# Expert rows through DRAM: tokens fetched by indirect DMA, results stored as rows and gathered back

## The reference, cut to what matters

```python
def moe_swiglu(h, router, w_gu, w_down):
    t = h.reshape(-1, shp[-1])                      # 256 tokens x 1024
    logits = (t @ router).astype(F32)
    top_v, top_i = lax.top_k(logits, TOP_K)         # 2 of 8 experts
    gates = jax.nn.softmax(top_v, axis=-1)
    combine = jnp.sum(jax.nn.one_hot(top_i, N_EXPERTS, dtype=F32) * gates[..., None], axis=1).astype(t.dtype)
    y = jnp.zeros_like(t)
    for e in range(N_EXPERTS):
        y = y + combine[:, e:e + 1] * swiglu(t, w_gu[e], w_down[e])
    return y.reshape(shp)
```

## Time and profile before

| | |
|---|---|
| median of 3 runs | 1613.47 us (1613.42 to 1613.71) |
| the profiled execution | 1617.29 us |
| its span, first to last instruction | 1615.5 us, mean granted TensorE clock 0.941 |
| PE busy | 1431.4 us (89%) |
| DVE, ACT, POOL busy | 892.8, 728.6, 91.0 us |
| DMA | 263.96 MB, mean 163 GB/s |
| eight expert passes | 1114.7 to 1590.3 us |
| in them: PE, DVE, ACT busy | 452.5, 383.9, 338.3 of 475.5 us, DMA share 0.82, 288 GB/s |

### The profile page before, as it was taken

One profiled execution on the slowest core, in us unless ns is written; L12 is line 12 of the kernel. 1 busy time (PEld: TensorE's weight loads), 2 busy tenths in 40 slices (PEclk: granted clock), 3 DMA queues, 4 the chain that ended last, 5 costly groups with the idle time before them and its releaser, 6 DMA issues.

```text
span 1615.5 us, 23095 instructions
## 1 busy us (share of the span) xinstructions
PE 1431.4 (89%) x8308; PEld 1150.2 (71%) x8308; DVE 892.8 (55%) x1387; ACT 728.6 (45%) x1076; POOL 91.0 (6%) x90
## 2 busy tenths in 40 slices
PE   5599978799889999999979945988999999999996
PEld 1377646356658888888848844667898888888884
DVE  0521276764352332233343486755887887887785
ACT  2322353454332321222132462543677677676774
POOL 2200010000030100011011010010000000000000
PEclk9699979899979999999988967998999999999998
DMA  8255544245212332223202510022887887887883
GB/s 318 77 196 188 202 146 168 104 183 182 79 40 97 115 102 80 91 91 126 83 30 88 167 56 0 1 69 103 303 283 284 304 296 277 303 302 271 300 307 124
DMA packets 69555, 263.96 MB, mean 163 GB/s; under 512 B 8112, under 2 KB 9552, under 8 KB 69360
## 3 DMA queue, kind: packets, MB, share of 16 engines
q1 hardware_dynamic: 68112, 259.55, 46.2%
q10 hardware_dynamic: 720, 2.30, 0.4%
q0 software_dynamic: 656, 1.18, 0.2%
HBM read 261.95 MB, written 1.05 MB: 163 GB/s over the span
## 4 chain that ended last, share of the span: by engine, by line
PE 71%; DVE 13%; ACT 7%; DMA 6%; issue 3%; POOL 0%; DVEq 0%; ACTq 0%; SPq 0%; POOLq 0%
PE ps L544 11%; PE ps L546 11%; PE ps L545 11%; DMA raw<-in_w_dn 3%; DVE wlo L460 3%; PE ps L880 3%; PE ps L884 3%; PE ps L882 3%; ACT whi L455 3%; PE ps L727 3%; PE ps L521 3%; PE ps L860 3%; PE ps L749 2%; PE ps L862 2%; PE ps L861 2%
## 5 line engine op out<-in xcount | busy, mean ns | idle before, releaser
L460 DVE TENSOR_TENSOR wlo<-raw,whi 128x1024 fp32r<-128x1024 f32 (+2 forms) x367 | 481.8, 1318 | 363.5 <-ACT whi L455 357.9
L455 ACT ACTIVATE whi<-raw 128x1024 fp32r<-128x1024 f32 (+2 forms) x367 | 411.8, 1124 | 370.0 <-PE ps L546 153.3
L544 PE MATMUL ps<-hhi,whi 128*128 128x512 f32 (+1 forms) x736 | 285.4, 388 | 40.1 <-POOL hlo L1275 38.7
L546 PE MATMUL ps<-hhi,wlo 128*128 128x512 f32 (+1 forms) x736 | 277.9, 378 | 0.0
L545 PE MATMUL ps<-hlo,whi 128*128 128x512 f32 (+1 forms) x736 | 277.4, 377 | 0.0
L860 PE MATMUL ps<-whi,hs_hi 128*128 128x256 f32 x704 | 207.9, 295 | 16.4 <-DVE wlo L460 12.6
L544 PEld LDWEIGHTS ps<-hhi,whi 128*128 128x128 f32 x736 | 141.7, 193 | 91.4 <-issue 37.2
L862 PE MATMUL ps<-whi,hs_lo 128*128 128x256 f32 x704 | 196.6, 279 | 0.0
L861 PE MATMUL ps<-wlo,hs_hi 128*128 128x256 f32 x704 | 196.6, 279 | 0.0
L545 PEld LDWEIGHTS ps<-hlo,whi 128*128 128x128 f32 x736 | 142.7, 194 | 25.2 <-issue 1.4
L546 PEld LDWEIGHTS ps<-hhi,wlo 128*128 128x128 f32 x736 | 142.7, 194 | 24.2
(11 more groups left out here) (251 smaller groups left out, 1928.2 us busy)
## 6 DMA issues: line engine op xcount, KB each, us to landing
raw<-in_w_gu SPq DMA_DIRECT2D x225, 512.0 KB, 4.4
raw<-in_w_dn SPq DMA_DIRECT2D x80, 704.0 KB, 6.1
raw<-in_w_mod SPq DMA_DIRECT2D x96, 512.0 KB, 4.2
raw<-in_w_fm SPq DMA_DIRECT2D x32, 512.0 KB, 3.4
raw<-in_w_out SPq DMA_DIRECT2D x16, 512.0 KB, 3.7
raw<-in_w_tg SPq DMA_DIRECT2D x8, 512.0 KB, 3.4
raw<-in_w_tv SPq DMA_DIRECT2D x8, 384.0 KB, 3.1
xT<-in_x ACTq DMA_DIRECT2D x1, 2048.0 KB, 12.0
```

The costliest lines, as they stand in the source:

```text
L455: nc.scalar.activation(whi[:, v % H, 0:cols], raw[:, slot, 0:cols], ACT.Copy).then_inc(hi_ready, 1)
L460: nc.vector.tensor_tensor(wlo[:, v % H, 0:cols], raw[:, place(v) % R, 0:cols], whi[:, v % H, 0:cols].bitcast(F32), ALU.subtract).then_inc( ...
L544: nc.tensor.matmul(outp, whs, xh, start=first, stop=False)
L546: return nc.tensor.matmul(outp, wls, xh, start=False, stop=last)
```

## The change

Tokens and results go through two DRAM tensors, and the matrices pair_w, scat and the sum yacc go.

- **h_rows** (256 x 1024): ACT stores both tiles of htm there before the first pass.
- **Slot to token.** tok holds each token's number (with the sign and offset that the constant matrix `before` gives). `slot_tokens(i)` on PE multiplies pair_in by tok, two products of one column, into bank 6, after j = 3 of the pass before; `slots_of(i)` on DVE turns the result into the integers slot_tok.
- **Fetch.** Pool fetches 128 rows of h_rows by indirect DMA into xg, once slot_tok is ready. `gather(i)` on PE now waits for xg and turns it by eight transposes into the same place of PSUM. pair(i + 1) on DVE moves from r == 9 to r == 3; slots_of(i + 1) stands at r == 9.
- **y_rows** (2048 x 1024): ACT stores ys there at the end of each pass, from its own queue, after it has waited for its copy. Its upper half is set to zero early, by Pool from back, before the norm ahead of the experts.
- **Back.** DVE works out slot_at, the two rows of y_rows that each token needs (`rows_of_tokens`), and wdiag, four diagonal matrices with the gate weights. After the last store Pool fetches two rows per token, four indirect DMAs of 512 KB; `rows_back` on PE multiplies them by wdiag, 32 full fp32 products, into banks 0 to 3, and DVE updates xT from PSUM.

The diff, cut to its core:

```diff
 @@ tensor
+            def slot_tokens(i):
+                pe.wait_ge(pair_ready, i + 1)
+                for t in range(2):
+                    mm = nc.tensor.matmul(ps[:, 6, 0:1], pair_in[:, t, :], tok[:, t:t + 1],
+                                          start=(t == 0), stop=(t == 1))
+                mm.then_inc(tok_done, 1)
             def gather(i):
-                pe.wait_ge(pair_ready, i + 1)
+                pe.wait_ge(xg_in, i * 16 + 16)
+                for k in range(KT):
+                    mm = nc.tensor.transpose(ps[:, 6 + k // 4, (k % 4) * P:(k % 4 + 1) * P],
+                                             xg[:, k * P:(k + 1) * P], ident[:, :])
+                mm.then_inc(gather_done, 1)
+            def rows_back():
+                pe.wait_ge(diag_ready, 4)
+                pe.wait_ge(back_in, 64)
                 for k in range(KT):
                     for t in range(2):
-                        mm = nc.tensor.matmul(ps[:, 6 + k // 4, (k % 4) * P:(k % 4 + 1) * P],
-                                              htm[:, t, k * P:(k + 1) * P], pair_in[:, t, :],
-                                              start=(t == 0), stop=(t == 1))
-                mm.then_inc(gather_done, 1)
-            def scatter(i, n):
...
+                        for w in range(2):
+                            mm = nc.tensor.matmul(
+                                ps[:, k // 2, (k % 2) * LAT + t * P:(k % 2) * LAT + (t + 1) * P],
+                                back[:, t, w, k * P:(k + 1) * P], wdiag[:, t, w, :], start=(w == 0), stop=(w == 1))
+                    if k % 2:
+                        mm.then_inc(sum_done, 1)
...
-                        if 1 <= j <= 4:
-                            scatter(i, j - 1)
-                        if j == 6:
-                            pe.wait_ge(pairw_ready, i + 1)
-                            for t in range(2):
-                                mm = nc.tensor.transpose(ps[:, 6, t * P:(t + 1) * P], pair_w[:, t, :], ident[:, :])
-                            mm.then_inc(scat_done, 1)
+                        if j == 3:
+                            slot_tokens(i + 1)
...
                         if u == 1:
-                            pe.wait_ge(scat_out, i + 2)
                             gather(i + 1)
-                for n in range(4):
-                    scatter(n_pass, n)
+                rows_back()
 @@ scalar
-                        if r == 13:
-                            act.wait_ge(scat_done, i + 1)
-                            nc.scalar.activation(scat[:, :], ps[:, 6, 0:LAT], ACT.Copy).then_inc(scat_out, 1)
...
                     act.wait_ge(split_used, i * BLOCK + (v0 + BLOCK))
+                    act.wait_ge(ys_used, i * 16 + 16)
                     nc.scalar.activation(ys[:, :], ps[:, 4:6, :].rearrange("p b n -> p (b n)"), ACT.Copy
                                          ).then_inc(ys_ready, 1)
+                    act.wait_ge(ys_ready, i + 1)
+                    act.dma_start(y_rows[bass.ds(i * P, P), :], ys[:, :]).then_inc(ys_used, 16)
...
+                act.wait_ge(htm_out, t + 1)
+                act.dma_start(h_rows[t * P:(t + 1) * P, :], htm[:, t, :]).then_inc(rows_out, 16)
 @@ gpsimd
+                def fetch(count):
+                    pool.wait_ge(rows_out, 32)
+                    pool.wait_ge(slot_ready, count)
+                    nc.gpsimd.indirect_dma_start(xg[:, :], None, h_rows[:, :], with_rows).then_inc(xg_in, 16)
+                fetch(1)
...
+                with pool.Fori(2, n_end) as n:
+                    fetch(n)
+                pool.wait_ge(at_ready, 1)
+                pool.wait_ge(ys_used, n_stored)
+                for t in range(2):
+                    for w in range(2):
+                        nc.gpsimd.indirect_dma_start(back[:, t, w, :], None, y_rows[:, :],
+                                                     bass.IndirectOffsetOnAxis(slot_at[:, t, w:w + 1], 0)
+                                                     ).then_inc(back_in, 16)
...
+            pool.wait_ge(mixlo[1], 4)
+            pool.wait_ge(alo_ready[1], len(att_tiles(1)))
+            nc.gpsimd.memset(back[:, 0, 0, :], 0.0).then_inc(zero_ready, 1)
+            pool.wait_ge(zero_ready, 1)
+            nc.gpsimd.dma_start(y_rows[NE * P:2 * NE * P, :].rearrange("(p a) n -> p a n", p=P),
+                                back[:, 0, 0:1, :].broadcast_to([P, NE, D])).then_inc(y_zeroed, 16)
             norm_lo(3)
+            experts()
 @@ vector
+            def slots_of(i):
+                dve.wait_ge(tok_done, i + 1)
+                V.tensor_copy(slot_tok[:, 0:1], ps[:, 6, 0:1]).then_inc(slot_ready, 1)
...
                 pair(0)
+                slots_of(0)
                 slots_lo(0)
+                rows_of_tokens()
...
-                        if r in (3, 5, 7, 9):
-                            add(i, (r - 3) // 2)
+                        if r == 3:
+                            pair(i + 1)
                         if r == 9:
-                            for t in range(2):
-                                ins = V.tensor_scalar(pair_w[:, t, :], slots[:, :], posx[:, t, bass.ds(i, 1)],
-                                                      pickx[:, t, bass.ds(i, 1)], ALU.is_equal, ALU.mult)
-                            ins.then_inc(pairw_ready, 1)
-                            pair(i + 1)
+                            slots_of(i + 1)
...
+                dve.wait_ge(sum_done, m // 2 + 1)
+                V.scalar_tensor_tensor(xT[:, m, CTX:T], ps[:, m // 2, (m % 2) * LAT:(m % 2 + 1) * LAT],
+                                       mod[:, 1, g:g + 1], xT[:, m, CTX:T], ALU.mult, ALU.add).then_inc(x_last, 1)
```

96 lines of the change are left out of this document (56 added, 40 removed).

## The result

The change made the kernel slower, by a little: **1619.11 us** (median of 20 runs) against 1613.2 for the kernel before on the same chip (20 runs); ratio 1.0040, 95% interval 1.0028 to 1.0052. The forecast was 1605, faster. The profiled execution took 1619.2 us, its span is 1617.4 at a granted clock of 0.931.

A forecast was written before the change was run, and what follows sets the result against it. No engine alone was taken as the limit: PE, DVE and DMA are all busy in the expert passes. Passes -21.6, step +2 and end +11 gave -8.6 us, so 1605 us, range 1597 to 1613 (chance 0.50).

The forecast's parts named there:

- The end: After the last pass: store, four fetches, 32 products and later squares replace the scatters; +11 us (+6 to +18).
- The passes: Eight expert passes: scatter -3.0, gather -2.5, ACT's store +0.7, traffic +1.7, small things +0.4; -2.7 each, -21.6 us.
- the store on ACT's queue: Pass start: ACT waits for its copy and issues a DMA before the table load; +0.7 us a pass (0.46 to 1.5).
- The step: From router into the passes: products, Pool's issue, landing and transposes replace the first gather; +2 us (0 to +9).
- The bounds of traffic: Per pass, one store and one fetch of 524,288 bytes plus faster weight loads: 0 to 3.6 us, taken as +1.7.
- The scatter term: Pairs j = 2 to 10 of a pass: without scatters 29.47 us falls to nine pairs at 2.95; -3.0 us a pass.
- While Pool works, DVE can be slowed: In a pass, Pool's fetch issue may slow one wlo on DVE by up to 1.5 us; within small things, +0.4.
- Every added byte is paid: Rival: the fetch shifts all later weight loads, traffic +3.6 us a pass, 1620 us in all; chance 0.22.
- The rate does not rise: Rival: five slots yield only today's 293 GB/s, +3.3 us a pass, 1652 us in all; chance 0.05.
- The rows come late: Rival: in the passes the gather becomes a wait for fetched rows, some 1645 us with 5 over; chance 0.05.
- Spare DMA: Rival: idle DMA share takes both transfers, pairs run at 2.95 us, -4.8 a pass, 1588 us; chance 0.18.
- Its signs: Wrong if: pass over 57.9 us, whi waiting for in_w_gu over 2 a pass, transposes waiting for xg, end over 18.

The follow-up runs named there:

- the second trace of before: The kernel before, unchanged, run and profiled once more: span 1613.6 us, median 1614.2 us.
- store_pool: The full change, but ys is stored from Pool's queue, behind its fetch, instead of from ACT's: 1610.2 us, ratio 0.9983 to the kernel before.
- sp_no_fetch: The change with results stored from Pool's queue, without the fetches inside the passes (first rows turned again each pass): 1599.1 us, ratio 0.9925 to the kernel before.
- g_only: The kernel before with only the fetch and eight transposes, results still by scatter, slot copy at r = 13: 1619.3 us, ratio 1.0040 to the kernel before.
- sp_warm: The change with results stored from Pool's queue, plus 16 unused products in PE's idle time before the final 32: 1611.2 us, ratio 0.9985 to the kernel before.

## Why the prediction was wrong, point by point

Forecast -8.6 us, measured +5.9 (medians): 14.5 too low. Three terms of its sum failed, and one mechanism that no term held. The end, +11, was +17.2: four fetches took 9.4 us and not 7.0, and the last square ends 3.9 and not 1.7 behind the 32 products. The passes, -21.6, were -15.9: the store on ACT's queue was taken at 0.7 a pass and was worth 1.1 to 1.3. The step, +2, was +4.7: rows fetched by index landed after 6.8 us, not 3.4 to 4.4. And no term held what follows a wait of PE, a stretch at half clock. By its own terms, against the second trace of before:

| term | forecast | measured | short by |
|---|---|---|---|
| eight passes | -21.6 | -15.9 | 5.7 |
| step into the passes | +2 | +4.7 | 2.7 |
| end | +11 | +17.2 | 6.2 |

**Right.** The gather as eight transposes: -2.5 a pass forecast, -2.4 measured at the down units. The first scatter gains nothing, as it said: PE waits 0.8 in its place in most passes. The zeroing of y_rows: landed 18.7 us after 1051.0, long before it is needed. The bounds of traffic, 0 to 3.6, held: 1.2 for the fetch, for which the 1.7 had counted some 1.0.

**Passes: the store on ACT's queue.** The three parts of a pass were put at +0.7 (start), -0.9 (third pair to the down units: -3.0 + 1.7 + 0.4) and -2.5; measured +0.9, -0.5 and -2.4. With the store on Pool's queue (store_pool) they are 0, -0.8 and -2.5: -3.3 in all, where the forecast without its store term is -3.4. So it is this term that was mis-sized. Its 1.00 of idle time on ACT lies in the stated bounds (0.46 to 1.5); the whole store was worth 1.3 a pass by the traces and 1.1 by the medians, so 3 to 5 of the 5.7 us. (Passes of one code differ by 0.7 between traces, so the medians, 8.9 us apart, carry more weight here.)

**Passes: scatter and pace.** The scatter term of -3.0 took 2.95 us as the pace of nine pairs, though the DMA share was 1.00 in the last two; the 0.7 in the traffic term answered for that. Without the fetch (sp_no_fetch) the nine pairs take 27.3 where they took 29.6, -2.3, which is the -3.0 with the 0.7 taken off it; in that is 0.5 for slot_tokens (pair 3 takes 3.4, its neighbours 2.9), put at 0.2 with the copy. PE's wait ahead of the down units grows by 0.3, so the whole stretch is 29.1 against 31.1. The fetch takes 1.2 of these 2.0. "DMA: Bandwidth & Descriptors" of the Trainium skill, section Issuing engines are not separate DMA queues, says that DMAs of all issuing engines run on the same 16 and interleave; the traces agree: in g_only a fetch on Pool's queue puts the down loads of SP's queue from 6.3 to 7.8.

**What no term held: the clock.** I wrote that the granted clock is 1.00 in the passes, and costed each new wait at its length. In the change 17 us of the passes run at half clock, each stretch behind a wait of PE. g_only's two passes price it, 2.5 us of 6.8 at half clock. In the change pair 9 takes 4.5 us in the four passes where it runs at half clock and 3.0 to 3.1 in the others, 1.4 more; but the down units behind it then run without waits, and passes 2, 6 and 7, which have such a stretch, are only 0.7 longer than passes 3, 5 and 8. From these numbers I estimate 3 to 6 us for all five stretches, which overlaps with the price of the store. No run removes the half clock alone inside the passes, so its share stays open.

**"While Pool works, DVE can be slowed"**: nothing of it was seen beside an issue. The two wlo that overlap Pool's issue here (store_pool, POOL's and DVE's timelines) keep their 1.23, and of all wlo of 1024 columns in the passes none takes longer, in the change or in store_pool:

```profile
1307.39 1.19 POOL L1304 DMA_INDIRECT xg<-h_rows,slot_tok  x1 [18.00 <-DVE slot_tok L1747]
```

```profile
1306.53 1.22 DVE L472 TENSOR_TENSOR wlo<-raw,whi 128x1024 fp32r<-128x1024 f32 x1
...
1308.18 1.23 DVE L472 TENSOR_TENSOR wlo<-raw,whi 128x1024 fp32r<-128x1024 f32 x1
```

The product xn in the earlier trace rows stood beside a subtraction of Pool; the term took an issue for the same kind of work, and the traces do not bear that out.

**Step.** The failed term is the landing: "3.4 to 4.4", from plain transfers of as many bytes; 128 rows by index took 6.8, and the hand-over to Pool 0.8 beside its issue. The products and the copy took 1.3 for 0.7, the transposes 2.0 for up to 2.6. The wider bound (+9) held. No run tests this step by itself.

**End.** Four fetches were put at 0.54 each and 5.8 for the bytes, 7.0 in all by the rate of weight loads; measured 9.4: each issue takes 0.94 and they follow at 1.24, and the rate from 1583.0 to 1592.4 is 223 GB/s, not 362. +2.4. "DVE's updates of xT now run beside it; squares end 1.7 later" became 3.9, +2.2: the last squares wait for the norm sums, which PE does after the products. The store took 0.4 more than put. And the base was too long: the 5.54 of the earlier trace rows stood partly at half clock and lasted 1.6 us longer than the same products in the second trace. The 9.8 for the 32 products (9.4) was right, with its reason: sp_warm shows the half clock as the cause of 2 us. Together 0.4 + 2.4 + 2.2 - 0.4 + 1.6 make the 6.2.

**The rivals.** "Every added byte is paid" put the turn to slower at a pass of 57.9 with an end of 13 in all. The passes stayed under that (57.5) and the kernel is slower nevertheless, because step and end cost 22 and not 13: its mechanism was half right, its time of 1620 hit for another reason. That hit is luck. "The rate does not rise" fell: 320 GB/s against 293. "The rows come late" fell: the transposes never wait for xg inside the passes. "Spare DMA" fell.

**Its signs.** Of the four by which it would be wrong one came: whi waits for in_w_gu 3.3 us a pass (23.0 in seven), over 2. A pass of 57.5 (57.9), an end of 17.2 (18) and the wait for xg did not come. Two slips in the working, of little weight: 9 x 0.07 is 0.6 and not 0.7, and 7.4 less 2.4 is 5.0 where the rival of every byte says 4.5.
